# Loop head slot, and the small state tables turned by VectorE in blocks of 32, in a hybrid decoder layer

## The reference

```
n1 = rmsnorm(x);  proj = n1 @ w_in            # z, xbc, dt, sc_b, sc_c, sc_h, gates
xbc_c, xbc_state = causal_dwconv(xbc, xbc0)   # 4 taps, 6144 channels: last 3 rows kept
y, h_new = ssd_scan(...)                      # 64 heads, 8 groups
branch_a = norm(y * silu(z)) @ w_ssm_out
sc_conv, sc_state = causal_dwconv(sc_c*sc_h, sc0)   # 3 taps, 2048 channels: last 2 rows
branch_b = (sc_b * sc_conv) @ w_sc_out
x = x + (sigmoid(ga)*branch_a + sigmoid(gb)*branch_b) @ w_o
g_conv, ffn_state = causal_dwconv(n2 @ w_ffn_gate, ffn0)  # 3 taps, 5632 channels
x = x + (silu(g_conv) * (n2 @ w_ffn_up)) @ w_ffn_down
x = x + (pe @ w_ple) * sigmoid(n3 @ w_ple_gate)
```

## Time and profile before

| | us |
|---|---|
| median of 3 runs | 2818.85 |
| the profiled execution | 2820.08 |
| its span in the profile | 2818.3 |
| TensorE busy (PE) | 2786.8, 99% |
| DVE busy | 1778.4, 63% |
| ACT busy | 1170.4, 42% |
| POOL busy | 300.1, 11% |

### The profile page before, as it was taken

How to read it: one execution, slowest core, us unless ns; L and a number is a source line. 1 busy time by engine, 2 the same in 40 slices (tenths; PEclk the granted TensorE clock), 3 DMA queues, 4 the chain that set the end, 5 groups by cost and what they waited for, 6 DMA issues and landing times.

```text
span 2818.3 us, 53398 instructions
## 1 busy us (share of the span) xinstructions
PE 2786.8 (99%) x19400; PEld 2755.6 (98%) x19400; DVE 1778.4 (63%) x2246; ACT 1170.4 (42%) x1726; POOL 300.1 (11%) x456
## 2 busy tenths in 40 slices
PE   8999999999999999999999999999999999999998
PEld 7899999999999999999999999999999999999998
DVE  7878877887888645555455556555555555555464
ACT  5554444544544333333333335433333333333553
POOL 3222221212222100000000001000000000000100
PEclk9999999999999999999999999999999999999999
DMA  8787887878878665555555554555555555555463
GB/s 224 206 206 191 215 222 194 204 207 207 220 185 210 183 192 150 149 146 149 151 150 151 149 149 130 165 150 149 149 149 149 149 149 149 149 149 149 135 182 112
DMA packets 903137, 477.18 MB, mean 169 GB/s; under 512 B 158441, under 2 KB 896673, under 8 KB 902705
## 3 DMA queue, kind: packets, MB, share of 16 engines
q1 hardware_dynamic: 828417, 433.15, 56.8%
q10 hardware_dynamic: 73936, 40.03, 5.1%
q0 software_dynamic: 672, 2.66, 0.2%
HBM read 449.95 MB, written 25.79 MB: 169 GB/s over the span
## 4 chain that ended last, share of the span: by engine, by line
PE 96%; DVE 1%; SPq 1%; ACT 0%; issue 0%; DMA 0%; ACTq 0%; DVEq 0%
PE ps L1797 30%; PE ps L1798 30%; PE ps L1799 30%; PE ps L2054 1%; PE ps L1952 1%; PE ps L1905 1%; PE ps L1953 1%; PE ps L2070 0%; PE ps L1962 0%; SPq L633 0%; PE ps L2188 0%; PE ps L2195 0%; DMA xrow<-in_x_sample 0%; DVE wlo L1149 0%; PE ps L2199 0%
## 5 line engine op out<-in xcount | busy, mean ns | idle before, releaser
L1797 PE MATMUL ps<-n_hi,whi 128*128 128x320 f32 x4144 | 1286.0, 310 | 4.7 <-issue 2.0
L1799 PE MATMUL ps<-n_hi,wlo 128*128 128x320 f32 x4144 | 1281.1, 309 | 0.0
L1798 PE MATMUL ps<-n_lo,whi 128*128 128x320 f32 x4144 | 1281.1, 309 | 0.0
L1149 DVE TENSOR_TENSOR wlo<-raw,whi 128x1024 fp32r<-128x1024 f32 x746 | 921.1, 1246 | 472.1 <-ACT whi L756 471.2
L756 ACT ACTIVATE whi<-raw 128x1024 fp32r<-128x1024 f32 x746 | 784.8, 1058 | 839.8 <-PE ps L1799 721.7
L1797 PEld LDWEIGHTS ps<-n_hi,whi 128*128 128x128 f32 x4144 | 778.6, 188 | 8.3 <-issue 2.8
L1798 PEld LDWEIGHTS ps<-n_lo,whi 128*128 128x128 f32 x4144 | 778.5, 188 | 1.3
L1799 PEld LDWEIGHTS ps<-n_hi,wlo 128*128 128x128 f32 x4144 | 778.4, 188 | 0.0
L1797 PE MATMUL ps<-c_hi,whi 128*128 128x320 f32 x1728 | 535.7, 310 | 0.7 <-DVE c_lo L1272 0.5
L1799 PE MATMUL ps<-c_hi,wlo 128*128 128x320 f32 x1728 | 533.9, 309 | 0.0
L1798 PE MATMUL ps<-c_lo,whi 128*128 128x320 f32 x1728 | 533.9, 309 | 0.0
(11 more groups left out here) (308 smaller groups left out, 1762.2 us busy)
## 6 DMA issues: line engine op xcount, KB each, us to landing
raw<-in_w_in SPq DMA_DIRECT2D x322, 512.0 KB, 4.7
raw<-in_w_ffn_gate SPq DMA_DIRECT2D x88, 512.0 KB, 4.4
raw<-in_w_ffn_up SPq DMA_DIRECT2D x88, 512.0 KB, 5.0
raw<-in_w_ffn_down SPq DMA_DIRECT2D x88, 512.0 KB, 4.0
raw<-in_w_ssm_out SPq DMA_DIRECT2D x64, 512.0 KB, 6.1
hs<-in_state_ssm ACTq DMA_DIRECT2D x32, 512.0 KB, 5.5
hq<-in_state_ssm SPq DMA_DIRECT2D x512, 32.0 KB, 3.3
out_ssm_sample<-hs ACTq DMA_DIRECT2D x32, 512.0 KB, 3.6
```

Source lines behind the costliest of these rows:

```text
L1149: tt(wlo[slot][:], raw[slot][:], whi[slot][:].bitcast(F32), SUB).then_inc(lo_split, 1)
L1797: mm(out, w_h, x_h, start=first, stop=False)
L1798: mm(out, w_h, x_l, start=False, stop=False)
L1799: return mm(out, w_l, x_h, start=False, stop=last)
```

## The change

Four things. The head of TensorE's `ssm` loop is placed at slot 48, not 0. The ffn's state table is loaded straight into `fstate` in four DMAs with runs of 32 values, and one DVE transpose turns it in place; TensorE's six turns and DVE's two copies go. The tails of x and of the short convolution are turned in place by two DVE transposes at the end of the first ffn step, and go out in 20 DMAs with runs of 128 bytes, two behind each weight load of `ffnend`; `xtail` gets 16 columns ahead of it so that the border between prompt and samples falls on a multiple of 32 (16 + 144 = 160). TensorE's turns, now the 7 blocks of `ftail` alone, move to the out steps 2 and 3.

```diff
-        xtail = fixed("xtail", [P, NB + 1, K_X - 1, XBC // P])
+        X_PAD = 16
+        xtail_mem = fixed("xtail_mem", [P, X_PAD + (NB + 1) * (K_X - 1) * (XBC // P)])
+        xtail = xtail_mem[:, X_PAD:].rearrange("p (i k t) -> p i k t", i=NB + 1, k=K_X - 1)
...
-                               head_slot={eng.engine: 0})
+                               head_slot={eng.engine: 48})
...
-        TAILS = [(xtail, 0, (NB + 1) * (K_X - 1) * (XBC // P), "xbc"),
-                 (stail, 11, (NB + 1) * (K_SC - 1) * KM, "sc"),
-                 (ftail, 14, (NB + 1) * (K_F - 1) * (DFF // P), "ffn")]
+        TAILS = [(ftail, 0, (NB + 1) * (K_F - 1) * (DFF // P), "ffn")]
...
+        def block_stores(table, pad, n_prompt, name):
+
+            for out_name, lo, hi in ((name + "_prompt", pad, pad + n_prompt),
+                                     (name + "_sample", pad + n_prompt, pad + (NB + 1) * n_prompt)):
+                dst = outs[out_name][0].rearrange("b k (t f) -> (b k t) f", f=P)
+                for pc in range(4):
+                    rows, cols = slice(pc * HB, (pc + 1) * HB), slice(pc * HB, (pc + 1) * HB)
+                    first = -(-lo // HB) * HB
+                    if lo < first:
+                        yield dst[0:first - lo, cols], table[pc * HB + HB - (first - lo):(pc + 1) * HB, first - HB:first]
+                    yield (dst[first - lo:hi - lo, cols].rearrange("(r j) f -> j r f", j=HB),
+                           table[rows, first:hi].rearrange("j (r f) -> j r f", f=HB))
+        EARLY_STORES = (list(block_stores(xtail_mem, X_PAD, (K_X - 1) * (XBC // P), "xbc"))
+                        + list(block_stores(stail_flat, 0, (K_SC - 1) * KM, "sc")))
...
+                    if seg.name == "ffnend":
+                        if pos == 0:
+                            sp.wait_ge(tails_turned, 2)
+                        for dst, src in EARLY_STORES[2 * pos:2 * pos + 2]:
+                            sp.dma_start(dst, src).then_inc(tails_stored, 16)
...
-                        act.dma_start(fsrow[:, 0:5, :], ffn_past[0:5 * P].rearrange("(r p) f -> p r f", p=P)
-                                      ).then_inc(ftab_loaded, 16)
-                        act.dma_start(fsrow[0:64, 5, :], ffn_past[5 * P:5 * P + 64]).then_inc(ftab_loaded, 16)
+                        for pc in range(4):
+                            rows = slice(pc * HB, (pc + 1) * HB)
+                            act.dma_start(flat_of(fstate)[rows, :].rearrange("i (r f) -> i r f", f=HB),
+                                          ffn_past[:, rows].rearrange("(r i) f -> i r f", i=HB)).then_inc(ftab_loaded, 16)
...
-                        for n in range(2):
-                            dve.wait_ge(ftab_turned, n + 1)
-                            lo, hi = 4 * P * n, min(4 * P * (n + 1), NB * (K_F - 1) * (DFF // P))
-                            v.tensor_copy(fstate[:].rearrange("p r t -> p (r t)")[:, lo:hi],
-                                          ps[:, 2 + n, 0:hi - lo]).then_inc(ftab_kept, 1)
+                        dve.wait_ge(ftab_loaded, 64)
+                        v.transpose(flat_of(fstate), flat_of(fstate)).then_inc(ftab_kept, 1)
...
                     fin(seg, it, j)
+                    if seg.name == "ffn" and seg.start == 0 and j == 3:
+                        dve.wait_ge(xtail_kept, 6 * GROUPS)
+                        v.transpose(xtail_mem[:], xtail_mem[:]).then_inc(tails_turned, 1)
+                        dve.wait_ge(stail_kept, 16)
+                        v.transpose(stail_flat, stail_flat).then_inc(tails_turned, 1)
...
+            g_.memset(xtail_mem[:, 0:X_PAD], 0.0)
...
-                if j == 3:
-                    pe.wait_ge(ftab_loaded, 32)
-                    for n in range(6):
-                        rows = P if n < 5 else 64
-                        last = turn(ps[:, 2 + n // 4, (n % 4) * P:(n % 4) * P + rows], fsrow[0:rows, n, :],
-                                    ident[0:rows, 0:rows])
...
-                if j == 2:
+                if j == 0:
                     pe.wait_ge(stail_kept, 16 + DFF // P)
-                if j >= 4:
-                    pe.wait_ge(tail_kept, 4 * (j - 4) + 4)
...
-                    if seg.name == "ffnend" and j < len(TAIL_FOURS):
-                        turn_tails(j)
+                    if seg.name == "ffnend" and 2 <= j < 2 + len(TAIL_FOURS):
+                        turn_tails(j - 2)
```

More of the change, by code:

```diff
@@ L294, in hybrid_decoder @@
         free_b = acc_b[:].rearrange("p a b -> p (a b)")
-        fsrow = free_b[:, 32 * P:38 * P].rearrange("p (r f) -> p r f", f=P)
-        trow = free_b[:, 0:21 * P].rearrange("p (r f) -> p r f", f=P)
+        trow = free_b[:, 0:7 * P].rearrange("p (r f) -> p r f", f=P)
         perow = free_b[:, 21 * P:21 * P + 3 * PLE].rearrange("p (c f) -> p c f", f=PLE)
@@ L391, in hybrid_decoder @@
         sig_back = sem("sig_back")
-        post_zero, ftab_loaded, ftab_turned, ftab_kept = (
-            sem("post_zero"), sem("ftab_loaded"), sem("ftab_turned"), sem("ftab_kept"))
+        post_zero, ftab_loaded, ftab_kept = sem("post_zero"), sem("ftab_loaded"), sem("ftab_kept")
         pe_loaded, pe_turned, pe_kept, pe_hi, pe_ready, ple_kept, ple_added = (
@@ L397, in hybrid_decoder @@
         tail_turned, tail_kept, tails_stored = sem("tail_turned"), sem("tail_kept"), sem("tails_stored")
+        tails_turned = sem("tails_turned")
         gains_loaded, y_turned, y_gained = sem("gains_loaded"), sem("y_turned"), sem("y_gained")
@@ L566, in tail_stores, with flat_of @@
                             r += n
+        def flat_of(table):
+            return table[:].rearrange("p a b -> p (a b)")
+        def block_stores(table, pad, n_prompt, name):
[9 more added lines that the diff above has]
+                           table[rows, first:hi].rearrange("j (r f) -> j r f", f=HB))
+        stail_flat = stail[:].rearrange("p i k t -> p (i k t)")
+        EARLY_STORES = (list(block_stores(xtail_mem, X_PAD, (K_X - 1) * (XBC // P), "xbc"))
+                        + list(block_stores(stail_flat, 0, (K_SC - 1) * KM, "sc")))
+        N_STORES = len(EARLY_STORES) + len(list(tail_stores()))
         def hs_uses(g, j):
@@ L711, in _ @@
                 sp.wait_ge(hs_stored[i], 16 * GROUPS * HS_OF.count(i))
-            sp.wait_ge(tails_stored, 16 * len(list(tail_stores())))
+            sp.wait_ge(tails_stored, 16 * N_STORES)
             sp.wait_ge(y_stored, 16 * 4)
@@ L952, in tasks @@
                 elif kind == "out" and seg.name == "ffnend":
-                    if j < len(TAIL_FOURS):
-                        act.wait_ge(tail_turned, j + 1)
-                        bank, blocks = TAIL_FOURS[j]
+                    if 2 <= j < 2 + len(TAIL_FOURS):
+                        act.wait_ge(tail_turned, j - 1)
+                        bank, blocks = TAIL_FOURS[j - 2]
                         for m, rows in blocks:
@@ L1567, in tasks @@
                     if seg.start == 1:
-                        dve.wait_ge(tails_stored, 16 * len(list(tail_stores())))
+                        dve.wait_ge(tails_stored, 16 * N_STORES)
                         dve.wait_ge(gains_loaded, 16)
@@ L1771, in tasks @@
                         pool.wait_ge(sconv_done, 16 + 4 * it)
-                        pool.wait_ge(ftab_kept, 2)
+                        pool.wait_ge(ftab_kept, 1)
                         base = PARAMS["cf"][0]
@@ L2010, in turn_inputs @@
             def turn_inputs(j):
-                if j == 3:
-                    pe.wait_ge(ftab_loaded, 32)
-                    for n in range(6):
-                        rows = P if n < 5 else 64
-                        last = turn(ps[:, 2 + n // 4, (n % 4) * P:(n % 4) * P + rows], fsrow[0:rows, n, :],
-                                    ident[0:rows, 0:rows])
-                        if n in (3, 5):
-                            last.then_inc(ftab_turned, 1)
                 if j == 4:
@@ L2130, in tasks @@
                     if j == 0:
-                        pe.wait_ge(ftab_kept, 2)
+                        pe.wait_ge(ftab_kept, 1)
                     if j == 2:
```

## The result

The changed kernel takes 2829.02 us (median of 7 runs, 2827.25 to 2830.41), the kernel before 2819.24 us (7 runs). The ratio is 1.0033, 95% interval [1.0024, 1.0043]: some 9.8 us slower, where 6 us faster was forecast. The profiled execution took 2827.9 us, its span is 2826.2 us, 7.9 more than before.

A forecast was written before the change was run, and what follows sets the result against it. TensorE, busy 99% of the span, was taken as the bound. From 2820.08 us profiled, -2.01 - 1.53 - 1.54 - 0.94 = -6.02 gave 2814.06; the median lying 1.23 us lower, 2812.8 us was forecast, range 2811.3 to 2816.9.

The forecast's parts named there:

- the term of the short-convolution loop: TensorE's short-convolution loop, 48 slots later: may touch one block more; left to the rivals, nothing in the sum.
- C': Rival: short-convolution loop touches an eighth block, head pushed out each round; two back edges at 3.54 us, +7.08; chance 0.04.
- Entry of the ssm loop: Head at slot 48 needs no fetch at loop entry: -2.01 us idle and -1.53 us clock, -3.54 together.
- Turns: TensorE loses 14 tail turns in the out steps, -1.54 us, and six for the ffn's table, -0.94 us.
- Exit of the ssm loop: Next block must come in at the loop's end, boundary 48 instructions nearer; costed at 0, bounds 0 and +2.0 us.
- rival C: Boundary behind the loop's end is nearer, or the clock still falls once: +1 to +2 us, 2814.3 us; chance 0.09.
- DVE: Two added tail transposes, some 1.9 us behind the first ffn step's last c_lo; cost 0, bounds 0 and +1.
- The ffn's table: Its four DMAs land in about 5 to 36 us, wanted 13 us after issue; cost 0, bounds 0 and +3.
- Short stores: 6336 runs of 128 bytes in the last ffn segment, 34 ns each; weight loads fall behind but stay hidden; cost 0.
- rival D: Short stores hold up last ffn segment's weight loads; stall from 60 ns a run, +11.4 us at 100 ns; chance 0.05.

The follow-up runs named there:

- x8: x4 with the ssm loop's head at slot 8 instead of 48; 2818.91 us in one run.
- x10: x4 with the ssm loop's head at slot 24 instead of 48; 2813.25 us in one run.
- x5: x4 without the hint for the ssm loop's back edge; 2814.39 us, ratio 0.9982 against the kernel before.
- x11: x4 with the ssm loop's head at slot 96, its hint kept, so that it touches eight blocks; 2815.45 us in one run.
- x9: x4 with all 20 short stores behind the fifth weight load of the last ffn segment; 2815.44 us, ratio 0.9987 against the kernel before.
- x4: The changed kernel, ssm head still at slot 48, with TensorE's short-convolution loop head placed at slot 0; 2814.93 us, ratio 0.9981 against the kernel before.
- x6: The kernel before with only the short-convolution loop's head placed at slot 220 (eight blocks); 2826.81 us, ratio 1.0031.
- x7: The kernel before with only the short-convolution loop's head placed at slot 200 (seven blocks); 2821.75 us, ratio 1.0005.
- x12: x6 with a hint for the short-convolution loop's back edge; 2817.53 us in one run, beside 2816.68 for the kernel before.
- x2: The kernel before with the ssm loop's head at slot 48 and nothing else; 2830.03 us, ratio 1.0034.
- x1: The changed kernel with the ssm loop's head back at slot 0; 2819.64 us, ratio 0.9992 against the kernel before.
- x3: The changed kernel with the ssm loop's head at slot 64; 2817.43 us, ratio 0.9988 against the kernel before.

## Why the prediction was wrong

The failed step is the term of the short-convolution loop, which the sum has at nothing. The working says only that the loop "can come to touch one block more, see the rivals" and gives no count against it. It was this rival, C', with a chance of 0.04, that came true, and its price of 7.08 us was too low: it cost 12.16 us. The sum gave 2814.06 us for the profiled execution; of the 13.8 us that are missing, 12.2 are here and 1.4 at the exit of the ssm loop. The median of the runs lies 16.2 above the forecast, since it came out 1.1 us above the profiled execution this time, not 1.2 below. Point by point:

- **Entry of the ssm loop.** Right, place and cause: the block count in the earlier trace rows and the end of the code ahead "between slots 5 and 30" (9 to 24 by x8 and x10). That estimate took the fetch's start for the step over the boundary, and was in part luck: in other profiles a fetch starts up to 4.3 us behind the entry branch (x5, x11). -4.07 us measured for -3.54: idle time and clock, and the stop varies. In six profiles with the fetch at the entry TensorE stood still 2.0, 3.9, 1.6, 4.3, 3.8 and 0.9 us.
- **Turns.** Right to 0.01 us: -0.93 and -1.54 for -0.94 and -1.54.
- **Exit of the ssm loop.** Taken as 0 with bounds 0 and +2; it was +1.37, rival C. Behind the hinted loop the next block's fetch came only 2.8 to 4.4 us after the exit, at every slot tried, and the boundary is now nearer. In x5, without the hint, it had come in before the exit, and nothing stood still there.
- **Short-convolution loop.** Two errors. The chance: the head's slot could be counted in the program, and the ssm loop's seven blocks were no evidence for eight. Nothing in the working said what the hint did: the ssm loop is hinted, this one isn't. The price: 3.54 us an edge, taken from the one stall of the trace, where it was 5.69 and 6.47. TensorE stood still for 4.0 and 3.8 us of that, in two stops each, by my reading because the head lies some 12 slots before the end of its block and the next one is missing too; the rest is the clock (0.71 and 0.62 in the stretches above). The place was off by one round as well: the stops are at 1150 and 1268 us, not "near 1260 and 1375". 2820.08 - 4.07 - 0.93 - 1.54 + 1.37 + 12.16 is 2827.1 us; the profiled execution took 2827.9; the rest lies in the first 138 us, the six ssm rounds and the end.
- **DVE.** Right that nothing waits: from 1800 to 1900 us TensorE has no wait at all. The timeline of DVE after:

```profile
1812.50 0.49 DVE L1299 TENSOR_TENSOR c_lo<-chunk,c_hi 128x320 fp32r<-128x320 f32 x1 [0.54 <-ACT c_hi L919]
1812.91 1.54 DVE L1588 STREAM_TRANSPOSE xtail_mem<-xtail_mem 128x1312 f32<-128x1312 f32 x1
1814.37 0.44 DVE L1590 STREAM_TRANSPOSE stail<-stail 128x288 f32<-128x288 f32 x1
1814.73 1.18 DVE L1176 TENSOR_TENSOR wlo<-raw,whi 128x1024 fp32r<-128x1024 f32 x1
```

  1.98 us for some 1.9. They stand at 1813 us, not near 1885: I had taken the end of the first loop round for the end of the step ahead of the loop. The split behind them has the same cover, so nothing hung on it.
- **The ffn's table.** Right, and with more room than thought. The lines of tile `fstate`, with the landing of its four DMAs:

```profile
L1526 DVE STREAM_TRANSPOSE fstate<-fstate x1: 903/903/903, 1731.4 to 1731.4; 128x704 f32<-128x704 f32 x1
...
DMA to landing us min/median/max: 2.5/2.6/2.7
```

  0.90 us for 0.85, and 2.6 us to land each, where 5 to 36 were the bounds.
- **Short stores.** Right that they cost nothing, with a price of 34 ns a run that was over twice too high. A run of 128 bytes took 13.2 ns (x9), a packet of 512 bytes 30.0 ns (the kernel before, 2300 to 2400 us): a quarter of the bytes for 0.44 of the time. So a short run did not cost more than a long one, and was far from the 60 ns from which rival D has TensorE stall. What a stream of such stores alone would cost no run shows.

The parts of the change are worth having. With the later loop placed as well and the hint left out, the same edits give 0.9982 [0.9973, 0.9990] (x5), 4 to 5 us faster than before. The version with the ssm head at slot 24 and the other at slot 0 took 2813.25 us in its one run (x10); the lowest runs of x4 and x5 are as low, so nothing shows that it is better.

## What to carry to other kernels

Whoever moves code ahead of a loop moves every loop behind it. Before such an edit, count each loop's instructions and its head's slot: what mattered here was whether a round came to touch an eighth block without a hint, and 20 slots decided it (rounds of 116.68 and 115.91 us in x6, of 112.64 in x7). And when a stall is priced from the one example in a trace, ask whether the new place would have it once or twice (3.54 us in that example, 5.69 and 6.47 at the new place).

## What the runs showed of the hardware

- Across a hinted back edge, loops that touch eight blocks of 256 instructions ran on without a fetch: six rounds in 672.16 us in x11 and rounds of 112.64 us in x12, with 52 fetches in all (one run each). Without a hint loops of seven did so: 672.17 us in x5 (51 fetches), 112.64 us in x7 (52). With eight and no hint every block was fetched anew in each round, 18 fetches in two rounds and 115.9 to 120.0 us a round (x6, x2, the changed kernel). I read this as eight blocks kept, of which the block behind the loop takes the eighth place where there is no hint. What nine do with a hint was not tried.
- At the entry a missing block stopped the sequencer for 2.6 to 5.9 us and TensorE for 0.9 to 4.3 us (3.73 and 2.01 us in the kernel before); over the rest TensorE worked on what was already queued. The stop varied by a factor of over two between executions, and mostly with the fetch's start: 0.2 to 0.3 us behind the branch it was 2.6 to 3.7 us (the kernel before, x6, x12), 3.0 to 3.5 us behind it 5.4 to 5.9 us (x1, x7, x8). Without it the runs of one kernel lie closer: 2813.0 to 2815.3 in x5, while the kernel before had 2816.4 to 2824.5 on the same chip.
- At its exit the hinted ssm loop left TensorE idle for 0.4 to 2.4 us at slots 48 and 64 (the changed kernel, x2, x3, x4, x9), where the next boundary is some 40 and 24 instructions away, and not at slots 0, 8 and 24, not with eight blocks (x11), and not without the hint (x5). At slot 48 it went with the fetch's start behind the exit branch: 2.8 us and 0.4 us idle (x4), 3.6 and 1.2 (x9), 3.9 and 1.5 (the changed kernel). Why that start varies stays open.
- Two stops of 2.0 us within 5.0 us, and of 2.6 and 1.2 us within 5.5 us, went with a mean granted clock of 0.71 in 5.8 us (from just ahead of the second stop on) and of 0.62 in 8.9 us (from the end of the first stop on); a single stop of 2.0 us at the entry before was followed by 0.66 in 5 us.
